# Seven raw weight buffers in place of six in an expert loop, assigned by piece

## What is computed

```python
gu = xb @ w_gu[e] + b_gu[e]            # xb: rows of one expert; w_gu[e]: 1024 x 2048, float32
g, up = jnp.split(gu, 2, axis=-1)
g = jnp.minimum(g, SWIGLU_LIMIT)
up = jnp.clip(up, -SWIGLU_LIMIT, SWIGLU_LIMIT)
glu = g * jax.nn.sigmoid(g * SWIGLU_ALPHA)
y = ((up + 1.0) * glu) @ w_down[e] + b_down[e]   # w_down[e]: 1024 x 1024
```

## Time and profile before

| | us |
|---|---|
| median of 3 runs | 1839.64 (1837.64 to 1841.82) |
| profiled execution | 1847.35, its span 1845.4 |
| mixer phase, to about | 430 |
| expert loop, 32 units, about | 430 to 1816 |
| closing sums and norm | 1816 to 1845 |

### The profile page before, as it was taken

The page is one execution under the profiler, slowest core; times in us unless marked ns, Lnnn a source line. Parts: engine busy times, 40 slices in busy tenths (PEclk is TensorE's granted clock), DMA queues, the critical chain, the costliest instruction groups (busy, mean ns, idle before and its releaser), DMA issues. The chain is left out here.

```text
span 1845.4 us, 29049 instructions
## 1 busy us (share of the span) xinstructions
PE 1698.6 (92%) x8545; PEld 1257.0 (68%) x8546; DVE 1327.8 (72%) x1137; ACT 1093.5 (59%) x1043; POOL 526.7 (29%) x376
## 2 busy tenths in 40 slices
PE   4989969956999999999999999999999999999977
PEld 4766658845577677777777777667667667665564
DVE  6487653556678696988977888669768668764776
ACT  5234363425577576767757677558556657663663
POOL 5222140331142161521322412126212126222220
PEclk8999979967999999999999999999999999999989
DMA  8210202238689898999988998779878788777783
GB/s 267 81 35 23 90 13 103 93 138 324 231 346 343 291 338 318 375 380 375 373 317 334 376 367 327 294 290 387 304 265 295 271 321 329 275 280 268 259 306 127
DMA packets 114067, 485.79 MB, mean 263 GB/s; under 512 B 16318, under 2 KB 28928, under 8 KB 81248
## 3 DMA queue, kind: packets, MB, share of 16 engines
q1 hardware_dynamic: 96016, 445.58, 63.0%
q0 software_dynamic: 18000, 39.49, 8.6%
HBM read 451.79 MB, written 33.23 MB: 263 GB/s over the span
## 5 line engine op out<-in xcount | busy, mean ns | idle before, releaser
L1442 DVE TENSOR_TENSOR w_lo<-raw_weights,w_hi 128x2048 fp32r<-128x2048 f32 x256 | 576.7, 2284 | 145.5 <-ACT w_hi L1298 145.4
L1298 ACT ACTIVATE w_hi<-raw_weights 128x2048 fp32r<-128x2048 f32 x256 | 485.8, 1911 | 228.4 <-PE ps L1595 121.0
L1593 PE MATMUL ps<-w_hi,xT 128*128 128x512 f32 x1024 | 415.0, 405 | 21.4 <-issue 12.1
L1594 PE MATMUL ps<-w_lo,xT 128*128 128x512 f32 x1024 | 402.4, 393 | 0.0
L1595 PE MATMUL ps<-w_hi,xT 128*128 128x512 f32 x1024 | 401.7, 392 | 0.0
L1442 DVE TENSOR_TENSOR w_lo<-raw_more,w_hi 128x2048 fp32r<-128x2048 f32 x128 | 290.2, 2286 | 50.9 <-ACT w_hi L1298 50.5
L1593 PEld LDWEIGHTS ps<-w_hi,xT 128*128 128x128 f32 x1024 | 193.8, 189 | 101.0 <-issue 51.9
L1298 ACT ACTIVATE w_hi<-raw_more 128x2048 fp32r<-128x2048 f32 x128 | 244.5, 1911 | 20.1 <-PE ps L1595 11.7
L1224 POOL DMA_INDIRECT x_rows<-h_rows,next_list x33 | 73.7, 2234 | 623.8 <-issue 623.8
L1595 PEld LDWEIGHTS ps<-w_hi,xT 128*128 128x128 f32 x1024 | 193.8, 189 | 42.7
L1594 PEld LDWEIGHTS ps<-w_lo,xT 128*128 128x128 f32 x1024 | 194.2, 190 | 36.7
(11 more groups left out here) (294 smaller groups left out, 2251.8 us busy)
## 6 DMA issues: line engine op xcount, KB each, us to landing
raw_weights<-in_w_gu SPq DMA_DIRECT2D x192, 1024.0 KB, 7.8
raw_more<-in_w_gu SPq DMA_DIRECT2D x64, 1024.0 KB, 6.2
raw_weights<-in_w_down SPq DMA_DIRECT2D x64, 1024.0 KB, 9.2
raw_more<-in_w_down SPq DMA_DIRECT2D x64, 1024.0 KB, 12.0
rows<-in_x SPq DMA_DIRECT2D x12, 512.0 KB, 5.7
w_in_sb<-in_w_in SPq DMA_DIRECT2D x12, 512.0 KB, 4.5
raw_weights<-in_w_out SPq DMA_DIRECT2D x1, 4096.0 KB, 13.2
acc_rows<-region_c SPq DMA_DIRECT2D x8, 512.0 KB, 2.7
```

The costliest lines, as they stand in the source:

```text
L1298: S.activation(w_hi[:, j % RING, :], raw(j % RING), ACT.Copy).then_inc(hi_done, 1)
L1442: V.tensor_tensor(w_lo[:, j % RING, :], raw(j % RING), w_hi[:, j % RING, :].bitcast(F32), ALU.subtract).then_inc(lo_done, 1)
L1593: T.matmul(out, hi, hi_w, start=first, stop=False)
L1594: T.matmul(out, hi, lo_w, start=False, stop=False)
```

## The change

Raw buffers become seven, and a table assigns them: pieces 0 to 6 to buffers 0 to 6, pieces 7 to 11 to buffers 0 to 4. Buffers 5 and 6 thus hold one piece per unit (5 and 6), the others two. SP's loop starts at 7 instead of 6 and ends with the next unit's piece 6; each request holds for the piece that last had its buffer.

| request | holds for the low split of, before | after |
|---|---|---|
| 6 | 0 | 11 of the unit before |
| 7, 8, 9, 10, 11 | 1, 2, 3, 4, 5 | 0, 1, 2, 3, 4 |
| next 0, 1, 2, 3, 4 | 6, 7, 8, 9, 10 | 7, 8, 9, 10, 11 |
| next 5 | 11 | 5, behind next 4 in the queue |

The six `w_hi` and `w_lo` buffers, the order on ACT, DVE, TensorE and GpSimd, and the sizes of the transfers stay. For room, `hT_tail` now lies over `glu_tail`. At the loop's end `b_down` and the gain, in raw buffer 4, hold for piece 11 instead of 10.

```diff
@@ -46,6 +46,8 @@
 RING = 6
+BUFFERS = 7
+RAW_OF = (0, 1, 2, 3, 4, 5, 6, 0, 1, 2, 3, 4)
@@ -1052,7 +1054,7 @@
-    slot, signal = shared["raw"](p % RING), shared["raw_in"][p % RING]
+    slot, signal = shared["raw"](RAW_OF[p]), shared["raw_in"][RAW_OF[p]]
@@ -1073,7 +1075,7 @@
-        raw_more = sb("raw_more", [P, RING - RAW, PIECE])
+        raw_more = sb("raw_more", [P, BUFFERS - RAW, PIECE])
@@ -1088,7 +1090,6 @@
-        hT_tail = sb("hT_tail", [P, KT, TAILS, TAIL])
@@ -1096,6 +1097,7 @@
         glu_tail = sb("glu_tail", [P, TAILS, QUARTER])
+        hT_tail = nc.alloc_sbuf_tensor_at("hT_tail", [P, KT, TAILS, TAIL], F32, offset=nc.sbuf_base - TAILS * QUARTER * 4)
@@ -1143,6 +1145,11 @@
+        def landed(p, u):
+
+            uses = [q for q in range(NP) if RAW_OF[q] == RAW_OF[p % NP]]
+            return raw_in[RAW_OF[p % NP]], 16 * len(uses) * (u + p // NP) + 16 * (uses.index(p % NP) + 1)
@@ -1175,18 +1182,19 @@
-            for p in range(RAW, RING):
+            for p in range(RAW, BUFFERS):
                 load_piece(sp, dram, shared, first, p)
...
-                for j in range(RING, RING + NP):
+                for j in range(BUFFERS, BUFFERS + NP):
                     if j == RING + 2:
                         hold(sp, bias_done, u + 1, held["sp"])
                         load_bias(after)
-                    hold(sp, raw_used[j // RING - 1], RING * u + j % RING + 1, held["sp"])
-                    hold(sp, lo_done, NP * u + j - RING + 1, held["sp"])
+                    left_by = max(q for q in range(j) if RAW_OF[q % NP] == RAW_OF[j % NP])
+                    hold(sp, raw_used[left_by // RING], RING * u + left_by % RING + 1, held["sp"])
+                    hold(sp, lo_done, NP * u + left_by + 1, held["sp"])
@@ -1340,7 +1348,7 @@
-                        act.wait_ge(raw_in[j % RING], 16 * NP // RING * u + 16 * (j // RING + 1))
+                        act.wait_ge(*landed(j, u))
```

More of the change, by code:

```diff
@@ L1296, in split_hi @@
             def split_hi(j):
-                S.activation(w_hi[:, j % RING, :], raw(j % RING), ACT.Copy).then_inc(hi_done, 1)
+                S.activation(w_hi[:, j % RING, :], raw(RAW_OF[j % NP]), ACT.Copy).then_inc(hi_done, 1)
             def x_hi(item, half):
@@ L1441, in split_lo @@
                 dve.wait_ge(hi_done, before + j + 1)
-                V.tensor_tensor(w_lo[:, j % RING, :], raw(j % RING), w_hi[:, j % RING, :].bitcast(F32),
+                V.tensor_tensor(w_lo[:, j % RING, :], raw(RAW_OF[j % NP]), w_hi[:, j % RING, :].bitcast(F32),
                                 ALU.subtract).then_inc(lo_done, 1)
@@ L1602, in gate_up_tail @@
                 def gate_up_tail(k, t):
-                    pe.wait_ge(raw_in[k % RING], 32 * u + 16 * (k // RING + 1))
-                    piece = interleaved(raw(k % RING))
+                    pe.wait_ge(*landed(k, u))
+                    piece = interleaved(raw(RAW_OF[k]))
                     for g in range(t):
@@ L1639, in down_tail @@
                 def down_tail(p, t):
-                    pe.wait_ge(raw_in[p % RING], 32 * u + 16 * (p // RING + 1))
-                    piece = raw(p % RING).rearrange("p (k n) -> p k n", k=2)
+                    pe.wait_ge(*landed(p, u))
+                    piece = raw(RAW_OF[p]).rearrange("p (k n) -> p k n", k=2)
                     for g in range(t):
@@ L1757, in hymba_moe_kernel @@
             "gates": ctx.enter_context(nc.sbuf_tensor("gates", [P, TT, E], F32)),
-            "raw_in": [ctx.enter_context(nc.semaphore(f"raw_in{i}")) for i in range(RING)],
+            "raw_in": [ctx.enter_context(nc.semaphore(f"raw_in{i}")) for i in range(BUFFERS)],
         }
```

## The result

The changed kernel takes 1869.11 us (median of 4 runs, 1867.48 to 1872.41), the kernel before beside it 1840.73 us. The ratio is 1.0150, with a 95% interval of 1.0112 to 1.0188: 28 us slower. Its profiled execution took 1869.59 us with a span of 1867.6.

A forecast was written before the change was run, and what follows sets the result against it. In the expert phase TensorE and the DMA engines were both taken as nearly full. 18.8 + 3.0 - 8.1 + 3.6 = +17.3 us on 1839.64 gives 1856.9 us; own range 1849 to 1866, with rivals 1842 to 1871.

The forecast's parts named there:

- rival 2: Half clock in nearly every (A) unit, ten stretches at 1.7 us: +31 us, 1870 us; chance 0.13.
- (A): Ten no-tail units after no-tail units (3, 8 to 12, 15 to 17, 21): together +18.8 us before the clock term.
- The limit and the fixed chain: Unit is the larger of TensorE's 35.66 us and piece 10's split start plus 12.87 us; limit 22.8 us after unit start.
- The price of piece 4: In (A), piece 4 moves into the stretch before piece 10, which lands 2.15 us later (1.95 to 2.3).
- the seven with idle engines at T: (A) units with DMA engines idle at the previous unit's last low split (piece 11): 2.15 us each, 15.0 together.
- (C): Six tail units after no-tail units (4, 6, 13, 18, 24, 27): TensorE's wait for hid_tail goes, -8.1 us.
- (B): No-tail units after tail units (2, 5, 7, 14, 20, 23, 26, 31): +3.0 us together, unit 23 included.
- unit 23: No-tail unit after the unit with two tails, its split of piece 10 waiting for the DMA: pays 2.1 us.
- The clock: TensorE's longer waits before transpose_h(0) in (A): three half-clock stretches at 1.2 us each, +3.6 us; bounds none and 17.
- the two rows: Two earlier TensorE idle stretches: after 2.7 us half clock for 3.4 us, after 2.8 us full clock.
- Rival 1: Scatter held back in (A), so piece 10 lands at 22.9 us and TensorE binds: faster, 1820.1 us; chance 0.13.
- remark on too few buffers: Same gap in every turn read as too few buffers, supporting Rival 1's outcome; the forecast held empty buffers against it.

The follow-up runs named there:

- order_564: Changed kernel with only SP's queue reordered: the next unit's pieces 5 and 6 are requested ahead of 4; 1822.22 us, run again 1823.52 us.
- the second: Second profile of the kernel before, unchanged, taken in a follow-up run: span 1833.6 us; that run measured 1840.24 us.
- late4_six_buffers: Kernel before, six buffers, with one edit: the next unit's piece 4 is requested after the low split of piece 11, not 10; 1875.66 us.
- share_2_to_6: Changed kernel with other buffers shared: pieces 7 to 11 use buffers 2 to 6 instead of 0 to 4; 1876.77 us.
- own_6_then_5: own_buffer_6 with one edit: the next unit's piece 6 is requested ahead of 5; 1835.06 us.
- the filler: Changed kernel plus five unused matmuls right before TensorE's wait for hid in units without tails; 1868.37 us.
- room_only: Kernel before with room for seven raw buffers and hT_tail over glu_tail, but six buffers in use and requests as before; 1842.56 us.
- own_buffer_6: Changed kernel with pieces 7 to 11 sharing buffers 1 to 5, so only piece 6 has its own buffer; 1841.13 us, run again 1844.81 us.

## Why the prediction was right, and where it was off

The direction and the mechanism held: slower, by the piece that was moved behind T. The size was low, 28.4 us measured against 17.3. The 1869.1 us lie above the forecast's own range (1849 to 1866) and inside the one with the rivals, next to the 1870 of rival 2. That the two agree is in part luck: rival 2 had ten half-clock stretches at 1.7 us each, and there were eight at 1.3 in (A), while the rest came largely from units 1, 2 and 31, for which the sum had no term. Step by step:

- **The limit and the fixed chain.** Split 10 plus 12.87 us gave each unit of the kernel before. After, with the full clock, it still does: unit 10 took 38.06 us with its split at 25.19. Where the half clock fell on the chain it was longer, 14.2 us in unit 11. TensorE's own time in an (A) unit is a little under the 35.66 us taken from unit 14: 35.3 in order_564.
- **The price of piece 4.** The starts of split 10 in (A) moved by 17.8 us against the first profile and 20.1 against the second; 18.8 was the forecast. late4_six_buffers shows that the request is the cause, share_2_to_6 and own_6_then_5 that in units with a hole it is the idle engines. Unit 12 was counted among the seven with idle engines at T, though the share at its T was 1.01; it paid 1.5 us.
- **(C).** -8.1 forecast, -8.5 to -9.0 measured. The way was not quite the one forecast: split 8 doesn't wait for TensorE then. In unit 13 it still waits 2.1 us for its DMA, but starts 23.5 us after T instead of 25.6, and that is enough.
- **(B) and unit 23.** +3.0 forecast, +1.7 measured without units 2 and 31. Unit 5 paid 0.2, not 0.6; unit 23 paid 1.1 of 2.1.
- **The clock: the term that was mis-sized.** I took three stretches at 1.2 us, 3.6; there were eight, 10.3 us together. What each cost (1.3) was right, the number was not. The step that failed was the weighing of the two rows as about even. In the changed kernel all eight (A) units whose wait was 2.47 us or longer had the half clock after it, and the two with 1.90 and 2.03 had not. Rival 2, the half clock in nearly every such unit, was the nearer one in this term. The Trainium skill (TensorE: Matmul & The Clock Gate, HAM oscillation) describes a loop in which the wait for a DMA lowers the clock in every turn, and the trace agrees with it in eight turns of ten. A wait's length alone doesn't decide it: with the filler, waits of 2.52 and 3.04 us were followed by the full clock and one of 1.98 by the half. In share_2_to_6 even one of 3.27 us kept the full clock, and in room_only, with the requests of the kernel before, 1.97 and 2.20 us lost it.
- **Not foreseen: units 1, 2 and 31.** They take 9.5 us more than in the second profile of before. Units 2 and 31 hold 6.6 of it: 4.3 by the longer wait at their start, and the rest with the half clock, which follows that wait for 6.8 us in each instead of 3.4. The sum had no term for either. In the first profile unit 31's single stall of 9.4 us hid it.
- **Rival 1, the scatter gives way,** didn't come: the scatter's landing lay inside the stretch as before, and split 10 never came near 22.8 us. Its remark on too few buffers, from the Trainium skill (Perfetto Trace Analysis, Optimization Strategy), reads differently after the runs. The gaps may have to do with buffers, since order_564, which is rid of them, uses the seventh; no run tried six buffers in another order. But the buffer alone made them longer, and the order of the requests decided.

My profiled execution of the kernel before was 7.7 us over its median. I left the distance as it was; the one stall in unit 31 was most of it. Against the second profile the span grew by 34.0 us, against the first by 22.2, and the medians give 28.4.

Open: why unit 21 takes 3.5 us more in both kernels with a buffer for piece 6 alone and in own_6_then_5, though its neighbours don't. In own_buffer_6 split 10 is 1.8 us later there than in the second profile of before, and a half-clock stretch of 3.4 us after the wait makes up the rest; what delays the split isn't shown. That the wait at the start of units 2 and 31 is for TensorE's instructions is argued, if closely: no semaphore ended it, both units are the first of their kind after another kind, it ends at a fixed time after a transfer of the instruction queue starts, and unit 5 has it only where it has the transfer. No run changed that transfer alone. Open too is why the first profile of before departs from this, and what unit 1 spends its 2.9 us on.

## What to carry to other kernels

When transfers and matmuls are both near full, look for the stretches in which the DMA queue is empty, and judge a prefetch by what it does to them. A request that comes earlier into a full queue brings nothing; one that leaves a hole behind it costs most of its transfer time, here 1.8 to 2.0 us of 2.5 per unit. One request queue in order is held by its most delayed request: put those whose buffers are free ahead of it. After a change of buffers write down for each request the event that it waits for, and sort the queue by that.

## What the runs showed of the hardware

- Waits of TensorE of 2.5 to 4.2 us, once per 40 us, came with 3.4 us at the half clock in eight of eight cases of the changed kernel. Each cost 1.3 us on the path. Over all kernels here, waits between 1.97 and 3.3 us went both ways.
- Five matmuls whose result is not used, put ahead of such a wait, took the half clock away in all but one of the (A) units and saved 11 us there, in one profile.
- TensorE's wait at the first unit of another kind is 2.0 to 2.6 us when one transfer of 1 MB is requested at T, about 9 us ahead of its end, and 4.1 to 4.9 us when two or three are. It is 2.8 to 4.0 us with one when the DMA queue is full across T. It ends 4.8 to 5.2 us after a transfer of the instruction queue starts, in twelve of thirteen profiles.
